# A three-layer transformer stack on one core: a new order of the first loads, constant products on TensorE, and sines apart from their angles

## The reference

```
def first_block(x, ...):
    mix = token_mixer(x, w_in, b_forget, rel_bias, w_out)     # two attentions of 8 heads, then @ w_out
    x = layer_norm(2**0.25 * x + mix, ln1_g, ln1_b)
    u = conv3(x @ w_up)                                       # 1024 -> 2 * 2816
    ffn = (value * gelu(gate)) @ w_down                       # 2816 -> 1024
    return layer_norm(2**0.25 * x + ffn, ln2_g, ln2_b)

def second_block(x, positions, ...):
    y = retention_mla_layer(x, positions, ...)                # rotary tables: cos, sin of pos * inv
    x = layer_norm_2(2**0.5 * x + y, ln_g[0], ln_b[0])
    y = moba_layer(x, positions, ...)
    return layer_norm_2(2**0.5 * x + y, ln_g[1], ln_b[1])
```

## Time and profile before

| | us |
|---|---|
| median of 3 runs | 821.38 |
| lowest, highest | 820.64, 822.02 |
| the profiled execution | 821.49 |
| its span, first to last instruction | 819.7 |

### The profile page before, as it was taken

One profiled execution on the slowest core, in us unless ns is written; L12 is line 12 of the kernel. 1 busy time (PEld: TensorE's weight loads), 2 busy tenths in 40 slices (PEclk: granted clock), 3 DMA queues, 4 the chain that ended last, 5 costly groups with the idle time before them and its releaser, 6 DMA issues.

```text
span 819.7 us, 12104 instructions
## 1 busy us (share of the span) xinstructions
PE 767.2 (94%) x4530; PEld 651.9 (80%) x4530; DVE 517.0 (63%) x910; ACT 390.9 (48%) x645; POOL 78.4 (10%) x98
## 2 busy tenths in 40 slices
PE   6999997999999999798988999999999989999995
PEld 5986875999999878697778777777788867777774
DVE  4554667677777764774565465855574497567575
ACT  5554662665656453264445544343434333563650
POOL 0000000011111100011031000220000014004000
PEclk9999999899999999999999999999999999999999
DMA  9742343455656574165326336344666616435402
GB/s 332 282 154 79 112 138 138 154 190 171 203 165 197 170 279 141 55 217 181 105 93 196 110 103 205 123 143 147 205 225 190 200 52 210 151 114 168 156 27 78
DMA packets 37291, 130.28 MB, mean 159 GB/s; under 512 B 4401, under 2 KB 4657, under 8 KB 37105
## 3 DMA queue, kind: packets, MB, share of 16 engines
q1 hardware_dynamic: 36000, 125.04, 46.0%
q0 software_dynamic: 1232, 4.46, 1.7%
HBM read 128.43 MB, written 1.05 MB: 158 GB/s over the span
## 4 chain that ended last, share of the span: by engine, by line
PE 83%; DVE 9%; POOL 3%; ACT 2%; issue 2%; DMA 1%; DVEq 0%; SPq 0%; ACTq 0%
PE acc L792 25%; PE acc L794 23%; PE acc L793 23%; PE acc L903 2%; PE acc L977 2%; PE acc L922 1%; POOL rot L1538 1%; PE acc L942 1%; POOL rot L1539 1%; DVE small L1401 1%; DVE res L1425 1%; DVE res L1393 1%; PE acc L901 1%; DVE res L1435 1%; DMA res<-in_x 1%
## 5 line engine op out<-in xcount | busy, mean ns | idle before, releaser
L1205 DVE TENSOR_TENSOR w_lo<-raw,w_hi 128x1024 fp32r<-128x1024 f32 (+2 forms) x235 | 282.6, 1228 | 89.5 <-ACT w_hi L1061 89.4
L1061 ACT ACTIVATE w_hi<-raw 128x1024 fp32r<-128x1024 f32 (+2 forms) x235 | 237.5, 1036 | 73.6 <-PE acc L794 66.3
L792 PE MATMUL acc<-X_hi,w_hi 128*128 128x256 f32 x616 | 179.0, 291 | 3.9 <-DVE w_lo L1205 2.9
L793 PE MATMUL acc<-X_lo,w_hi 128*128 128x256 f32 x616 | 176.3, 286 | 0.0
L794 PE MATMUL acc<-X_hi,w_lo 128*128 128x256 f32 x616 | 176.1, 286 | 0.0
L792 PE MATMUL acc<-w_hi,X_hi 128*128 128x512 f32 (+1 forms) x352 | 141.7, 402 | 9.3 <-DVE X_lo L1212 4.5
L794 PE MATMUL acc<-w_hi,X_lo 128*128 128x512 f32 (+1 forms) x352 | 135.4, 385 | 0.0
L793 PE MATMUL acc<-w_lo,X_hi 128*128 128x512 f32 (+1 forms) x352 | 135.2, 384 | 0.0
L792 PEld LDWEIGHTS acc<-X_hi,w_hi 128*128 128x128 f32 x616 | 120.2, 195 | 8.5 <-issue 4.0
L793 PEld LDWEIGHTS acc<-X_lo,w_hi 128*128 128x128 f32 x616 | 120.4, 195 | 0.1
L794 PEld LDWEIGHTS acc<-X_hi,w_lo 128*128 128x128 f32 x616 | 120.2, 195 | 0.0
(11 more groups left out here) (147 smaller groups left out, 729.2 us busy)
## 6 DMA issues: line engine op xcount, KB each, us to landing
raw<-in_w SPq DMA_DIRECT2D x225, 512.0 KB, 4.2
raw<-in_w SPq DMA_DIRECT2D x8, 288.0 KB, 2.8
gate<-in_ln_gain POOLq DMA_DIRECT2D x4, 512.0 KB, 4.3
gate<-in_ln_bias POOLq DMA_DIRECT2D x4, 512.0 KB, 4.9
res<-in_x SPq DMA_DIRECT2D x4, 256.0 KB, 3.6
gate<-in_bias SPq DMA_DIRECT2D x1, 1024.0 KB, 10.3
out<-res SPq DMA_DIRECT2D x4, 256.0 KB, 2.1
decay<-in_decay SPq DMA_DIRECT2D x1, 512.0 KB, 10.3
```

The source lines that it names most:

```text
L792: nc.tensor.matmul(out, a_hi, b_hi, start=start, stop=False)
L793: nc.tensor.matmul(out, a_hi, b_lo, start=False, stop=False)
L1061: nc.scalar.activation(w_hi[:, u % RING, 0:n], raw[:, u % RAW, 0:n], ACT.Copy).then_inc(hi_done, 1)
L1205: nc.vector.tensor_tensor(w_lo[:, u % RING, 0:n], raw[:, u % RAW, 0:n], w_hi[:, u % RING, 0:n].bitcast(F32), ALU.subtract).then_inc(lo_don ...
```

## The change

In the list of steps, the four tiles of x are turned in another order (both token halves of feature half 0, then both of feature half 1), with the split of half of weight piece 0 ahead of them. Two new steps, `warm`, put products of a constant (an area set to 1.0) on PE: three ahead of the transposes and four behind them. Their results go to a bank that is overwritten later. The first half of piece 0 is loaded by a transfer that ACT issues; the second half and everything else stay with SP. `const` (the rest of it) and `b_forget` are issued after piece 5, the bias after piece 9, the positions, convolution and decay tables after piece 17. The step `tables` is cut in two: the angles stay where they were on DVE, and ACT's sines are emitted ahead of the down projection's ninth piece.

```diff
@@ plan(), run()
+            if half == (sines, 0):
+                emit(("sines",))
@@ plan()
     emit(("load", "start"))
-    for st in turn_x(0, 0) + turn_x(0, 1):
+    tok0, tok1 = turn_x(0, 0), turn_x(0, 1)
+    emit(("warm", 0))
+    emit(("split_hi", 0, 0))
+    emit(("split_lo", 0, 0))
+    for st in (tok0[0], tok1[0], tok0[1], tok1[1]):
         emit(st)
-    split_to(AHEAD)
+    emit(("warm", 1))
+    split_to(1)
@@
-    emit(("tables",))
+    emit(("angles",))
     emit(("load", "ln", 1))
     emit(("load", "even"))
-    run("down", 0, tail=turn_x(2, 0))
+    run("down", 0, tail=turn_x(2, 0), sines=8)
@@ SP
-                    for i in range(2 * NT):
-                        tt, q = divmod(i, 2)
+                    for tt, q in ((0, 0), (1, 0), (0, 1), (1, 1)):
                         sp.dma_start(res[:, tt, q * 512:(q + 1) * 512],
...
-                    for u in range(RAW):
+                    sp.dma_start(raw[:, 0, 512:1024], t["w"][0, :, 512:1024]).then_inc(landed[0], 16)
+                    for u in range(1, RAW):
                         load_piece(u)
-                        if u == 2:
-                            sp.dma_start(cst[:, P:], t["const"][:, P:]).then_inc(const_in, 16)
-                            sp.dma_start(bforget, t["b_forget"]).then_inc(bf_in, 16)
-                    sp.dma_start(bias[:, :, :], t["bias"]).then_inc(bias_in, 16)
-                    sp.dma_start(posi[:], t["positions_2"]).then_inc(pos_in, 16)
-                    sp.dma_start(cvp[:], t["conv"]).then_inc(conv_in, 16)
-                    sp.dma_start(decay[:], t["decay"]).then_inc(even_in, 16)
                 elif step[0] == "split_lo":
-                    if step[1] + RAW < NU:
+                    if len(step) == 2 and step[1] + RAW < NU:
                         load_piece(step[1] + RAW)
+                    if step == ("split_lo", 0):
+                        sp.dma_start(cst[:, P:], t["const"][:, P:]).then_inc(const_in, 16)
+                        sp.dma_start(bforget, t["b_forget"]).then_inc(bf_in, 16)
+                    elif step[1] == 4:
+                        sp.dma_start(bias[:, :, :], t["bias"]).then_inc(bias_in, 16)
+                    elif step[1] == 12:
+                        sp.dma_start(posi[:], t["positions_2"]).then_inc(pos_in, 16)
+                        sp.dma_start(cvp[:], t["conv"]).then_inc(conv_in, 16)
+                        sp.dma_start(decay[:], t["decay"]).then_inc(even_in, 16)
@@ PE
-                if part == 0:
+                if u == 0 and part == 0:
+                    pe.wait_ge(half_lo, 1)
+                elif u == 0 or part == 0:
                     pe.wait_ge(lo_done, u + 1)
...
+            def warm(n):
+                if n == 0:
+                    pe.wait_ge(half_ready, 1)
+                for _ in range((3, 4)[n]):
+                    nc.tensor.matmul(acc[:, 3, 0:256], fox[:, 3, 0:P], fox[:, 3, :], start=True, stop=True)
@@ ACT
+            act.dma_start(raw[:, 0, 0:512], t["w"][0, :, 0:512]).then_inc(half_landed, 16)
             for step in ORDER:
-                if step[0] == "split_hi":
+                if step == ("split_hi", 0, 0):
+                    act.wait_ge(half_landed, 16)
+                    nc.scalar.activation(w_hi[:, 0, 0:512], raw[:, 0, 0:512], ACT.Copy).then_inc(half_hi, 1)
+                elif step == ("split_hi", 0):
+                    act.wait_ge(landed[0], 16)
+                    nc.scalar.activation(w_hi[:, 0, 512:1024], raw[:, 0, 512:1024], ACT.Copy).then_inc(hi_done, 1)
+                elif step[0] == "split_hi":
                     split(step[1])
...
-                elif step[0] == "tables":
+                elif step[0] == "sines":
                     act.wait_ge(ang_done, 1)
@@ DVE
+                if step == ("split_lo", 0, 0):
+                    dve.wait_ge(half_hi, 1)
+                    nc.vector.tensor_tensor(w_lo[:, 0, 0:512], raw[:, 0, 0:512], w_hi[:, 0, 0:512].bitcast(F32),
+                                            ALU.subtract).then_inc(half_lo, 1)
...
-                elif step[0] == "tables":
-                    tables()
+                elif step[0] == "angles":
+                    angles()
@@ POOL
+            nc.gpsimd.memset(fox[:, 3, :], 1.0).then_inc(half_ready, 1)
             nc.gpsimd.memset(half_neg, -0.5).then_inc(pool_chain, 1)
-            nc.gpsimd.memset(fox[:, 3, :], 1.0).then_inc(half_ready, 1)
```

More of the change, by code:

```diff
@@ L258, in evacuate, with run @@
             given.add(name)
-    def run(name, rate, needs=lambda i: set(), early=0, between=(), tail=()):
+    def run(name, rate, needs=lambda i: set(), early=0, between=(), tail=(), sines=None):
         c = BY[name]
@@ L649, in build @@
         const_in, ident_in, bias_in = sem("const_in"), sem("ident_in"), sem("bias_in")
+        half_landed, half_hi, half_lo = sem("half_landed"), sem("half_hi"), sem("half_lo")
         x_in = [sem(f"x_in{i}") for i in range(2 * NT)]
@@ L762, in _ @@
                     sp.dma_start(ident, t["const"][:, 0:P]).then_inc(ident_in, 16)
[L763 to L764 removed]
+                    for tt, q in ((0, 0), (1, 0), (0, 1), (1, 1)):
                         sp.dma_start(res[:, tt, q * 512:(q + 1) * 512],
[L766 to L767 removed]
+                                     t["x"][0, tt * P:(tt + 1) * P, q * 512:(q + 1) * 512]).then_inc(x_in[2 * tt + q], 16)
+                    sp.dma_start(raw[:, 0, 512:1024], t["w"][0, :, 512:1024]).then_inc(landed[0], 16)
+                    for u in range(1, RAW):
                         load_piece(u)
[L769 to L775 removed]
                 elif step[0] == "split_lo":
[L777 removed]
+                    if len(step) == 2 and step[1] + RAW < NU:
                         load_piece(step[1] + RAW)
+                    if step == ("split_lo", 0):
[7 more added lines that the diff above has]
+                        sp.dma_start(decay[:], t["decay"]).then_inc(even_in, 16)
                 elif step == ("store",):
@@ L1005, in ret_o @@
                     .then_inc(ro_ready, 1)
+            def warm(n):
[3 more added lines that the diff above has]
+                    nc.tensor.matmul(acc[:, 3, 0:256], fox[:, 3, 0:P], fox[:, 3, :], start=True, stop=True)
             for step in ORDER:
-                if step[0] == "mm":
+                if step[0] == "warm":
+                    warm(step[1])
+                elif step[0] == "mm":
                     mm(step)
@@ L1370, in h_split, with angles @@
                 nc.vector.tensor_tensor(S_lo[:, j, :], hh[j % 2], S_hi[:, j, :].bitcast(F32), ALU.subtract).then_inc(h_lo, 1)
-            def tables():
+            def angles():
                 dve.wait_ge(pos_in, 16)
@@ L1470, in _ @@
             for step in ORDER:
-                if step[0] == "split_lo":
+                if step == ("split_lo", 0, 0):
+                    dve.wait_ge(half_hi, 1)
+                    nc.vector.tensor_tensor(w_lo[:, 0, 0:512], raw[:, 0, 0:512], w_hi[:, 0, 0:512].bitcast(F32),
+                                            ALU.subtract).then_inc(half_lo, 1)
+                elif step == ("split_lo", 0):
+                    dve.wait_ge(hi_done, 1)
+                    nc.vector.tensor_tensor(w_lo[:, 0, 512:1024], raw[:, 0, 512:1024], w_hi[:, 0, 512:1024].bitcast(F32),
+                                            ALU.subtract).then_inc(lo_done, 1)
+                elif step[0] == "split_lo":
                     split(step[1])
```

1 line of the change is left out of this document (removed).

## The result

| kernel | median us | lowest to highest | runs |
|---|---|---|---|
| before | 821.15 | 819.65 to 822.02 | 6 |
| changed | 815.57 | 814.12 to 815.91 | 5, and one of 4253.48 |

The median of all six is 815.59. The ratio without the one is 0.9932, with a 95% interval of 0.9915 to 0.9949. Five runs of the same file in a later series gave 814.82 (ratio 0.9917, 0.9904 to 0.9930). The profile read here is that of the later series: 814.62 us, span 812.8.

The account below looks back on a forecast made before the run. PE was taken as the bound, 83% of the span, so only its idle or low-clock time pays. Sines 2.0 plus start 0.5 made 2.5 us off 821.5: 819.0, or 818.9 against the median; 8-in-10 range 816.0 to 821.0.

Parts of the forecast that it names:

- (5): Start: the clock rises 5.5 us after 9.2, at 14.7; ten products of `f` are slow; 0.5 us gained.
- rival B: Start: clock high by the end of the transposes, closing constants take 1.7 us; 5.1 gained in all, 816.3 us; chance 0.20.
- effective start: When `f` would have started at the full clock, counting its slow products' loss: forecast 13.5 us against 14.0 before.
- The sines: Border before the down projection: DVE's low part, and PE with it, start 2.0 us earlier; the sines' new place costs nothing.
- rival E: Later stages: the clock falls at the third normalisation and one more stage end, 2.4 us each; 823.8 us; chance 0.07.
- (1): Start: three opening constant products take 2.6 us, about 1.1 to 3.7, before x is there, and delay nothing.
- (2): Loads at the start: the half piece beside x makes x 0.5 us late; last tile at 8.0, transposes done at 9.2.
- (3): Start: the half piece lands 3.3 to 7.6 us after issue; ACT's copies end by 11.3, before PE needs them.
- (4): Start: four closing constants take 3.4 us at the low clock, replacing the wait for the split; `f` starts at 12.6.
- (7): Start: the two extra halves of a split cost ACT and DVE a few tenths beside PE.
- (6): First attention: `b_forget` issued at 12.4, lands 7.5 later; piece 5 ready at 26.8, needed at 28.0; covered by 1.2 us.

Follow-up runs that it names:

- e2: The kernel before with only the sines moved, behind eight pieces of the down projection; 817.56 us, ratio 0.9954.
- e5: The kernel before, run again without an edit; 821.96 us, ratio 1.0012.
- e9: The kernel before with five constant products on PE ahead of the down projection's fifth piece, where PE stood idle; 821.36 us, ratio 1.0001.
- e10: e2 with five constant products on PE ahead of the down projection's fifth piece; 818.19 us, ratio 0.9976.
- e1: The changed kernel, run again without an edit; 814.82 us, ratio 0.9917.
- e3: The changed kernel without its seven constant products; 815.17 us, ratio 0.9914.
- e4: The changed kernel with the sines put back right behind the angles, so the new start alone; 818.96 us, ratio 0.9960.
- e7: The changed kernel without constant products, with the rest of `const` and `b_forget` issued behind piece 1; 813.28 us, ratio 0.9915.
- e8: The changed kernel with the first half of piece 0 issued by SP ahead of x, not by ACT; 815.68 us, ratio 0.9943.
- e11: e7 with five opening constant products and no closing ones; 814.28 us, ratio 0.9918.
- e12: e7 with the change's own three opening and four closing constant products; 815.43 us, ratio 0.9936.
- e6: The kernel before with three constant products in PE's idle time between the transposes and `f`; 820.17 us, ratio 0.9986.

## Why the prediction was wrong

**The step that failed is (5), the clock.** It counted 5.5 us from the end of the transposes (9.2) and let the rise come at 14.7, "because constant products are dense like those of `f`", and took from the kernel before that 16 transposes had done nothing. The rise came at about 10.2, 1.3 us after the transposes ended and 5.1 after they began: had the 5.5 us been counted from the start of the unbroken work (5.1), they would have given 10.6. What separates the two kernels is the idle time behind the transposes.

In all five profiles in which PE stood still for 2.89 to 3.18 us there (before, e2, e5, e9, e10), all 16 transposes and the beginning of `f` ran at the low level, and the change of spacing came between 15.4 and 17.1, 3.8 to 5.5 us after `f` began. In the seven in which PE had no such gap (e1, e3, e4, e7, e8, e11, e12), it came 3.1 to 5.7 us after the row of work began, with the transposes or, in e11, with the opening constants: in e11 near 5.2, in the others from 8.5 (e4) to 11.8 (e8). `f` was then at the high level from its second product on, but for e3, where ten products passed first. e3 and e7 have the same transposes and nothing ahead of them, and their rises lie 2.1 us apart, so a part of it is left to the execution. The eighth, e6, with 2.14 us of idle time, had the rise before its gap. e10 and e7 make the sharpest contrast: 16 transposes in one row, 2.89 us of idle time behind them in e10 and none in e7 (its rows stand above).

```profile
4.04 4.02 PE L963 MATMUL acc<-cst,res 128*128 128x128 f32 x16 [4.04 <-DMA res<-in_x]
10.95 0.58 PE L794 MATMUL acc<-X_hi,w_hi 128*128 128x256 f32 x1 [2.89 <-DVE w_lo L1211]
```

In e10 the rise came at 15.7, in e7 at 8.9. I had the idle time in front of me in the earlier trace rows, between 8.70 and 11.58, and used only its length.

So rival B, at a chance of 0.20, was right in its figure: closing products of 2.27 us (1.7 forecast there) and an effective start of 11.1 (10.9). In its condition it was early: the clock was not up at the end of the transposes, and x coming 0.3 us earlier than reckoned made up for part of that. The gain of the start is 3.0 in place of 0.5, and this term alone carries the forecast from 818.9 to 816.4. The Trainium skill, "TensorE: Matmul & The Clock Gate", section "What's actually happening", by which all of PE's recent work sets the gate, was weighed in the prediction and given too little; e7, where only transposes stood ahead of the rise, agrees with it. The same section warns that the number of slow products at a kernel's start differs between executions; the five profiles with the late rise agree, with 18 to 26 of them. My argument against it, the low clock at the first normalisation, was no argument: there PE idles between two groups of transposes, before's case again:

```profile
142.85 1.09 PE L961 MATMUL acc<-cst,res 128*128 128x128 f32 x4 [4.69 <-DVE res L1435]
```

**The sines: mechanism and wait right, the gain of the run too small.** The order of events, the wait (2.11 measured, 2.0 forecast), the rest that DVE leaves (0.28, forecast 0.4) and the free new place were as told, though the sines came 7.6 us later by the clock (292.21 against 284.57) and not 20. In the median the part gave 4.2. The other two microseconds are low stretches of the clock in the second and third layer: by the table under e5, the five profiles with the sines in the old place have two or three of them between the second and the third normalisation, the eight with the sines moved have one, but for e10 with none and e12 with two. That is 1.4 to 2.6 us between most of them, and it makes up what the wait leaves of the 4.2. I had this as rival E with the sign reversed, and dearer (2.4 us each, 0.9 to 1.6 measured): that a shift of later work could bring on falls, never that it could take some away. It rests on one profile per kernel. The place of the sines is also not all that decides: the kernel before itself took 817.3 to 817.9 us in three executions. What decides whether the clock falls in a given place stays open. It isn't the idle time at the border (e9); whether a plain shift in time by 2.1 us brings the falls back, e10 leaves open. Not tried was the kernel before with its sines in yet other places.

**Right:** (1) The opening constants are free: 2.93 us in the row, before x. (2) The first tile of x comes late by 0.6 (the forecast had 0.5, for the last tile), the transposes end at 8.87 (9.2). The Trainium skill, "DMA: Bandwidth & Descriptors", section "Issuing engines are not separate DMA queues", says that ACT's transfers meet SP's on the same engines; by it the half piece takes 0.8 from x. The trace has 0.63 at the first tile, so it agrees in kind. What e8 adds is that the place in the queue mattered more than the sharing: x was 2.1 us later than before when the half piece went first. (3) The half piece lands 3.4 us after issue, at the early end of 3.3 to 7.6. (4) The second half's low part was ready at 10.8 (11.2 forecast), and `f` started at 10.93 against 12.6: 1.1 of the 1.7 us are the clock's error, the rest is that the closing products could begin at 8.66 and not at 9.2. (7) Nothing was seen of the extra halves.

**(6) The tables: a cover thinner than told.** `b_forget` was issued at 11.7 (12.4) and landed 6.3 us later (7.5). Piece 5 was ready at 25.1 (23.86 + 1.23), and PE, earlier by the clock's error, didn't wait; with another 0.6 us (e4) or 1.3 us (e3) taken from the start it does (0.34 and 0.36 us). It was not a cost of the change but the next limit behind it: lifted, it let e7 keep what removing the constants gave, by the profile's norm 1; the ratios are too wide to show it.

## What to carry to other kernels

- When a slow clock follows an idle gap at the start, look at what PE did before the gap as well: here closing the gap (earlier inputs, in the order of need) let the clock rise at 8.9 or 11.0 us with no filler at all (e7, e3), against 8.5 to 11.8 with it and 15.4 to 17.1 with the gap. Filler that stands in the chain costs time as soon as nothing else is late (1.7 us at norm 1 in e12 against e7).
- Let small transfers that gate a later step (half a KB of bias) go out early; moving them behind large ones is safe only up to the slack of the step that waits.
- Where unrelated edits move a median by more than their wait explains, count the products in the stretches with a low granted clock, in more than one profile, before giving the difference to the edit.

## What was unexpected in the hardware

One execution out of six of the changed kernel took 4253.48 us; the five others of that series and the five of e1 took 814 to 816. Its page:

```profile
PE 4233.1 (100%) x4544; PEld 3264.5 (77%) x4544; DVE 518.9 (12%) x911; ACT 394.0 (9%) x646; POOL 77.9 (2%) x98
...
L802 PE MATMUL acc<-X_lo,w_hi 128*128 128x256 f32 x616 | 635.9, 1032 | 0.0
```

DVE and ACT are about as busy as ever (516.7 and 390.7 us in e1), while PE needs 1032 ns for a product that takes 284 in e1, from the first microseconds to the last, and the granted clock reads 1.00 throughout. It was not seen again in any run of this or another kernel; its cause is open.

The column of the granted clock reads 1.00 at the start although the spacing of products shows the low level (and e3 up to 11.03).
